# Group norm taken out of the chunk scan of a hybrid decoder layer, with paired first tiles at the projections' seams

## What is computed

```python
def ssd_mixer(xbc, dt_raw, z, h0, dt_bias, a_log, d_skip, g_norm, pad_front, chunk):
    ...
    y, h_last = ssd_scan(padt(xs), padt(dt), A, padt(Bm), padt(Cm), h0g, chunk)
    y = y[:, pad_front:pad_front + T] + d_skip...[:, :, None] * xs
    y = y.reshape(b, T, D_INNER) * jax.nn.silu(z.astype(f32))
    yg = y.reshape(b, T, SSD_GROUPS, D_INNER // SSD_GROUPS)
    yg = yg * lax.rsqrt(jnp.mean(yg * yg, axis=-1, keepdims=True) + EPS)
    y = yg.reshape(b, T, D_INNER) * g_norm.astype(f32)
    ...
mixed = jax.nn.sigmoid(ga) * (attn @ w_attn_out) + jax.nn.sigmoid(gs) * (ssd @ w_ssd_out)
x = x + mixed @ w_o
```

## Time and profile before

| what | value |
|---|---|
| median of 3 runs | 3813.21 us (3798.59 to 3815.85) |
| the profiled execution | 3804.04 us |
| its span from first to last instruction | 3802.2 us |
| PE busy | 3588.9 us (94%) |
| DVE, POOL, ACT busy | 2041.8, 1532.0, 811.5 us |
| mean granted TensorE clock | 0.951 of full speed |
| chain that ended last, by engine | PE 85%, DVE 6%, ACT 4%, issue 2%, DMA 1%, POOL 1% |

### The profile page before, as it was taken

One profiled execution on the slowest core, in us unless ns is written; L12 is line 12 of the kernel. 1 busy time (PEld: TensorE's weight loads), 2 busy tenths in 40 slices (PEclk: granted clock), 3 DMA queues, 4 the chain that ended last, 5 costly groups with the idle time before them and its releaser, 6 DMA issues.

```text
span 3802.2 us, 57123 instructions
## 1 busy us (share of the span) xinstructions
PE 3588.9 (94%) x22343; PEld 3397.6 (89%) x22343; DVE 2041.8 (54%) x3192; ACT 811.5 (21%) x1634; POOL 1532.0 (40%) x678
## 2 busy tenths in 40 slices
PE   7999999988999999996789989998999899999998
PEld 7999999988959999996789767668999799999998
DVE  5343333365759999876456534893165433433334
ACT  2000000022231111334565324662210200000000
POOL 2534435323313444442385004774433245344351
PEclk9999999999989999998799876999999999999999
DMA  2111111112202222222531215763242011111111
GB/s 86 56 39 44 55 33 54 45 45 62 59 28 84 89 95 80 98 89 62 69 112 51 66 42 132 190 163 117 96 143 71 23 50 55 39 44 55 33 55 56
DMA packets 399860, 272.33 MB, mean 72 GB/s; under 512 B 61850, under 2 KB 375538, under 8 KB 399736
## 3 DMA queue, kind: packets, MB, share of 16 engines
q1 hardware_dynamic: 379912, 225.76, 21.6%
q10 hardware_dynamic: 19824, 44.95, 3.1%
HBM read 211.05 MB, written 59.81 MB: 71 GB/s over the span
## 4 chain that ended last, share of the span: by engine, by line
PE 85%; DVE 6%; ACT 4%; issue 2%; DMA 1%; POOL 1%; SPq 1%; ACTq 0%; DVEq 0%; POOLq 0%
PE setA L349 10%; PE setA L350 10%; PE setA L351 10%; PE setB L349 9%; PE setB L350 9%; PE setB L351 9%; PE bankC L349 2%; PE bankC L351 2%; PE bankC L350 2%; PE bankD L351 2%; PE bankD L349 2%; PE bankD L350 2%; PE bankC L1417 2%; PE setA L1435 2%; PE setB L1435 2%
## 5 line engine op out<-in xcount | busy, mean ns | idle before, releaser
L341 POOL TENSOR_TENSOR whi<-wraw,ones 128x1024 fp32r<-128x1024 f32 x192 | 464.3, 2418 | 1688.2 <-PE setA L351 1078.3
L349 PE MATMUL setA<-hhi,whi 128*128 128x352 f32 (+1 forms) x2304 | 758.9, 329 | 43.2 <-issue 15.0
L350 PE MATMUL setA<-hlo,whi 128*128 128x352 f32 (+1 forms) x2304 | 751.2, 326 | 0.0
L351 PE MATMUL setA<-hhi,wlo 128*128 128x352 f32 (+1 forms) x2304 | 749.9, 325 | 0.0
L349 PE MATMUL setB<-hhi,whi 128*128 128x352 f32 (+1 forms) x2304 | 746.3, 324 | 0.0
L350 PE MATMUL setB<-hlo,whi 128*128 128x352 f32 (+1 forms) x2304 | 742.3, 322 | 0.0
L351 PE MATMUL setB<-hhi,wlo 128*128 128x352 f32 (+1 forms) x2304 | 741.1, 322 | 0.0
L349 PEld LDWEIGHTS setA<-hhi,whi 128*128 128x128 f32 x2304 | 441.1, 191 | 52.1 <-issue 25.8
L344 POOL TENSOR_TENSOR wlo<-wraw,whi 128x1024 fp32r<-128x1024 f32 x192 | 473.3, 2465 | 15.0
L350 PEld LDWEIGHTS setA<-hlo,whi 128*128 128x128 f32 x2304 | 441.0, 191 | 2.0
L351 PEld LDWEIGHTS setA<-hhi,wlo 128*128 128x128 f32 x2304 | 440.6, 191 | 0.0
(11 more groups left out here) (415 smaller groups left out, 5835.6 us busy)
## 6 DMA issues: line engine op xcount, KB each, us to landing
wraw<-in_w_in SPq DMA_DIRECT2D x64, 512.0 KB, 3.6
wraw<-in_w_ffn_gate SPq DMA_DIRECT2D x44, 512.0 KB, 3.7
wraw<-in_w_ffn_up SPq DMA_DIRECT2D x44, 512.0 KB, 3.7
wraw<-in_w_ffn_down SPq DMA_DIRECT2D x44, 512.0 KB, 3.5
abc<-acsD SPq DMA_DIRECT2D x8, 2048.0 KB, 9.8
xcD<-cv ACTq DMA_DIRECT2D x24, 520.0 KB, 2.7
xc<-xcD SPq DMA_DIRECT2D x8, 1536.0 KB, 14.4
zD<-spill ACTq DMA_DIRECT2D x16, 524.0 KB, 2.7
```

Of the source, the lines that this page charges most:

```text
L341: pool.tensor_tensor(dst_cols(slot, hi), dst_cols(slot), ones[:, :].unsqueeze(1).to_broadcast([P, KD, P]), ALU.mult).then_inc(w_hi, 1)
L349: pe.matmul(out, w1, r1, start=start, stop=False)
L350: pe.matmul(out, w1, r2, start=False, stop=False)
L351: return pe.matmul(out, w2, r1, start=False, stop=stop)
```

## The change

- `norm` leaves the scan. ACT copies the sums of squares of every chunk into rows `sums` (4 groups by 1048 tokens), and after the scan it takes two roots of 2 x 1048 elements a partition. DVE takes two reciprocals of the same size, each behind two of the state copies.
- y is written over z in `zc`; `y2` and `ss4` go. z has a semaphore of its own (`z_loaded`) that only the first `gate` of a chunk waits for. SP's `turn` loads `abc`, `xc` and `tc`, stores y unnormalised, waits until the store has landed, and then loads z.
- The 8 sample tokens aren't normalised on their own either: their root, reciprocal and product go, and their sums join `sums`.
- `dve_rows` multiplies `sraw` by gain and reciprocal in place (24 instructions for a half), ahead of the seam. The rounding at the seams is then one instruction a piece on ACT and one on DVE.
- The second `sraw` load is issued after the second SO weight load instead of the fourth.
- `gemm_pair` makes the first two tiles at all three seams, and waits for the second split only ahead of its second tile.
- Some semaphores of the sample part become the engine's common chain; ACT's loop over chunks is written out.

The diff, cut to what the text speaks of:

```diff
@@ -369,11 +369,13 @@
 
         def gemm_pair(pe, n, q, ready, between=None):
 
-            pe.wait_ge(w_split, n + 2)
+            pe.wait_ge(w_split, n + 1)
             for c, (o, w) in enumerate(CH):
                 if ready is not None:
                     pe.wait_ge(ready[0], ready[1] + c + 1)
                 for j in range(2):
+                    if j and c == 0:
+                        pe.wait_ge(w_split, n + 2)
                     if q:
                         pe.wait_ge(gemm_evac[j], 3 * (q - 1) + c + 1)
                     for k in range(KD):
...
@@ -1650,8 +1649,6 @@
             act.wait_ge(s_sc, 2 * NS + 2)
             act.activation(ps_[:, 0:PAST + 1], ss_[:, 0:PAST + 1], ACT.Exp, bias=smn[:, 0:1], scale=-1.0,
                            accum_out=smn[:, 1:2]).then_inc(s_relu, 1)
-            act.wait_ge(ys_ss, 2)
-            act.activation(rss[:, :, :], rss[:, :, :], ACT.Sqrt, bias=eps[:, 0:1], scale=1.0 / GW).then_inc(smp_act, 1)
...
-            v.wait_ge(smp_act, 2)
-            ch.run(v.reciprocal(rss[:, :, :], rss[:, :, :]))
-            v.tensor_tensor(ys[:, :, :].rearrange("p (g k) b -> p g k b", g=SG),
-                            ys[:, :, :].rearrange("p (g k) b -> p g k b", g=SG),
-                            rss[:, :, :].unsqueeze(2).to_broadcast([P, SG, GB, NS]), ALU.mult).then_inc(smp_norm, 1)
...
-        a = Region(AR, mboff - AR)
-        y2 = a.take("y2", [P, 2, NXB, P])
-        a = Region(mboff, AEND - mboff)
-        a.cur += DI * 4
-        zc = a.take("zc", [P, 2, NXB, P])
+        zc = at("zc", [P, 2, NXB, P], F32, mboff + DI * 4)
+        sums = at("sums", [P, SG, T], F32, mboff + DI * 4 + 2 * NXB * P * 4)
...
@@ -1885,46 +1874,53 @@
                 sp.dma_start(xc[slot][:, :, 0:w], xcD.rearrange("(b p) t -> p b t", p=P)[:, :, ts])\
                     .then_inc(chunk_loaded[slot], 16)
 
-            def load_rest(c, slot):
+            def load_tok(c, slot):
                 o, w = tok0(c)
-                ts = bass.ds(o, w)
-                sp.dma_start(tc[0:w, slot, :], tokD[ts, :]).then_inc(chunk_loaded[slot], 16)
-                sp.dma_start(zc[:, slot, :, 0:w], zD.rearrange("(b p) t -> p b t", p=P)[:, :, ts])\
-                    .then_inc(chunk_loaded[slot], 16)
-
-            def load(c, slot):
-                load_in(c, slot)
-                load_rest(c, slot)
-
-            def step(c, slot, used, nxt):
+                sp.dma_start(tc[0:w, slot, :], tokD[bass.ds(o, w), :]).then_inc(chunk_loaded[slot], 16)
+
+            def load_z(c, slot):
                 o, w = tok0(c)
-                sp.wait_ge(norm_ready, c * SG + SG)
-                sp.dma_start(sD.rearrange("(b p) t -> p b t", p=P)[:, :, bass.ds(o, w)], y2[:, slot, :, 0:w])\
+                sp.dma_start(zc[:, slot, :, 0:w], zD.rearrange("(b p) t -> p b t", p=P)[:, :, bass.ds(o, w)])\
+                    .then_inc(z_loaded[slot], 16)
+
+            def store_rows(c, slot):
+                o, w = tok0(c)
+                sp.dma_start(sD.rearrange("(b p) t -> p b t", p=P)[:, :, bass.ds(o, w)], zc[:, slot, :, 0:w])\
                     .then_inc(slot_out[slot], 16)
+
+            def turn(c, slot, used, nxt):
+
+                sp.wait_ge(y2_ready, c * SG + SG)
+                if nxt is not None:
+                    load_in(nxt, slot)
+                    load_tok(nxt, slot)
+                store_rows(c, slot)
+                if nxt is not None:
+                    sp.wait_ge(ysq_ready, c * SG + SG)
+                    sp.wait_ge(slot_out[slot], used * 16 + (SSD_OUT1 + 16))
+                    load_z(nxt, slot)
...
+            turn(0, 0, 0, 2)
             with sp.Fori(0, (NCH - 3) // 2) as i:
-                sp.wait_ge(y2_ready, i * 8 + 8)
-                load(i * 2 + 3, 1)
-                step(i * 2 + 1, 1, 0, None)
-                sp.wait_ge(y2_ready, i * 8 + 12)
-                load(i * 2 + 4, 0)
-                step(i * 2 + 2, 0, 0, None)
-            step(NCH - 2, 1, 0, None)
+                turn(i * 2 + 1, 1, i, i * 2 + 3)
+                turn(i * 2 + 2, 0, i + 1, i * 2 + 4)
+            turn(NCH - 2, 1, 0, None)
+            turn(NCH - 1, 0, 0, None)
             load_ao(sp, 2)
-            step(NCH - 1, 0, 0, None)
+        rs23 = at("rs23", [P, 2, T], F32, AR + 2 * XB)
...
             def ssq_copy(c, g, slot):
                 w = width(c)
                 wait_u(act, ssq_done, c, g, 0)
-                if g == 0 and not (isinstance(c, int) and c < 2):
-                    act.wait_ge(norm_ready, c * SG - SG)
-                act.activation(ss4[:, slot, g, 0:w], bankD[:, 0:w], ACT.Identity).then_inc(ssq_copied, 1)
-                if g == SG - 1:
-                    act.wait_ge(ssq_copied, c * 4 + 4)
-                    act.activation(ss4[:, slot, :, 0:w], ss4[:, slot, :, 0:w], ACT.Sqrt, bias=eps[:, 0:1],
-                                   scale=1.0 / GW).then_inc(root_done, 1)
+                o, _ = tok0(c)
+                act.activation(sums[:, g, o:o + w], bankD[:, 0:w], ACT.Identity).then_inc(ssq_copied, 1)
...
+            act.activation(sums[:, :, L:T], rss[:, :, :], ACT.Identity).then_inc(rss_in, 1)
             exps(0, 0, 0, 0)
-            over_chunks(act, step)
+            for c in range(NCH):
+                step(c, c % 2, c // 2, c + 1 if c < NCH - 1 else None)
             part_high(2, 4 * NCH)
             ssq_copy(NCH - 1, SG - 2, 0)
             square(NCH - 1, SG - 1, 0)
             ssq_copy(NCH - 1, SG - 1, 0)
+            act.wait_ge(ssq_copied, 4 * NCH)
+            act.wait_ge(rss_in, 1)
+            for h, dst in enumerate((sums[:, 0:2, :], rs23[:, :, :])):
+                act.activation(dst, sums[:, 2 * h:2 * h + 2, :], ACT.Sqrt, bias=eps[:, 0:1], scale=1.0 / GW)\
+                    .then_inc(root_done, 1)
...
-                if g == 0 and not (isinstance(c, int) and c < 2):
-                    v.wait_ge(slot_out[slot], used * 16 + SSD_OUT1)
+                if g == 0:
+                    v.wait_ge(z_loaded[slot], used * 16 + 16)
                 bs = slice(GB * g, GB * g + GB)
-                v.tensor_tensor(y2[:, slot, bs, 0:w], SETS[s][:, 0, :].rearrange("p (b t) -> p b t", t=P)[:, :, 0:w],
+                v.tensor_tensor(zc[:, slot, bs, 0:w], SETS[s][:, 0, :].rearrange("p (b t) -> p b t", t=P)[:, :, 0:w],
                                 zc[:, slot, bs, 0:w], ALU.mult).then_inc(y2_ready, 1)
 
...
-            def norm(c, slot):
-
-                w = width(c)
-                v.wait_ge(root_done, c + 1)
-                v.wait_ge(y2_ready, c * 4 + 4)
-                v.reciprocal(ss4[:, slot, :, 0:w], ss4[:, slot, :, 0:w]).then_inc(rstd_ready, 1)
-                v.wait_ge(rstd_ready, c + 1)
-                for g in range(SG):
-                    bs = slice(GB * g, GB * g + GB)
-                    v.tensor_tensor(y2[:, slot, bs, 0:w], y2[:, slot, bs, 0:w],
-                                    ss4[:, slot, g:g + 1, 0:w].to_broadcast([P, GB, w]), ALU.mult).then_inc(norm_ready, 1)
...
-                    if g == 2 and not (isinstance(c, int) and c == 0):
-                        norm(c - 1, 1 - slot)
...
-            norm(NCH - 1, 0)
-            for m in range(NXB // 4):
-                v.wait_ge(fin_done, m + 1)
-                v.tensor_copy(fin_st[:, m, :, :], CD[m % 2][:, :].rearrange("p (b n) -> p b n", n=P))\
-                    .then_inc(fin_evac, 1)
+            v.wait_ge(slot_out[1], Y_OUT0[1])
+            for h, t_ in enumerate((sums[:, 0:2, :], rs23[:, :, :])):
+                for m in (2 * h, 2 * h + 1):
+                    v.wait_ge(fin_done, m + 1)
+                    v.tensor_copy(fin_st[:, m, :, :], CD[m % 2][:, :].rearrange("p (b n) -> p b n", n=P))\
+                        .then_inc(fin_evac, 1)
+                v.wait_ge(root_done, h + 1)
+                v.reciprocal(t_, t_).then_inc(rstd_ready, 1)
...
             for m in range(KD):
                 load_tile(sp, TILE_SO + m, 0, m % 2, col_tile(so[0:D, :], m * P))
-                if m == 3:
+                if m == 1:
                     sp.wait_ge(part_ready, 6)
                     sp.dma_start(sraw[:, :, :], sD[D:2 * D, :].rearrange("(k p) t -> p k t", p=P)).then_inc(sraw_loaded, 16)
...
             for s in (1, 2, 3):
                 n, q = (TILE_AO + 8 * s, PART_ORD[s])
-                for m in range(2):
-                    gemm_tile(pe, n + m, q, m, ready=(part_ready, 3 * s) if m == 0 else None)
+                gemm_pair(pe, n, q, (part_ready, 3 * s))
                 with pe.Fori(0, 3 if s < 3 else 2) as i:
                     for j in range(2):
                         gemm_tile(pe, i * 2 + (n + 2 + j), i + (q + 1), j)
...
-        def act_high(act, s, c):
+        def act_high(act, s, src, c):
 
             o, w = CH[c]
-            act.wait_ge(mix_ready, 3 * (KD - 1) + c + 1)
+            if s < 3:
+                act.wait_ge(rows_ready, 3 * (s - 1) + c + 1)
+            else:
```

(40 more changed lines are left out.)

50 lines of the change are left out of this document (24 added, 26 removed).

## The result

The change takes **3775.5 us** (median of 4 runs, 3770.4 to 3781.8), the kernel before 3814.0 beside it: ratio 0.9909 (95% interval 0.9879 to 0.9938). In a later group of runs it took 3780.4 against 3803.1, ratio 0.9936 (0.9919 to 0.9954). It is faster by 0.6 to 0.9%. The profiled executions differ by less than the first medians (38.5 us): 3804.04 - 3776.31 = 27.7 us.

The account below looks back on a forecast made before the run. Scan bound by PE's work plus the wait for input. 27.9 + 1.0 + 1.5 + 7.0 - 8.6 + 4.6 + 5.6 = 39.0 us took the profiled 3804.0 to 3765.0, carried to the median as 3774; range 3755 to 3797.

Parts of the forecast that it names:

- The forecast case: Whole kernel: the terms come as summed, median 3774 us, own range 3762 to 3785; chance 55%.
- Scan, 27.9: Scan's 22 steps: `front` no longer waits for z, so PE keeps 6.57 us a step; 27.9 us gained.
- The 0.7 us kept for the boundaries: Scan: loss still allowed at the six chunk boundaries together, in case the input lands later; 0.7 us.
- The rival that DVE and POOL would hold PE at 7.0 us a step: Scan: without the norm's pause DVE and POOL slow PE, 9 us lost; chance 17% together with late input.
- z's room, 7 us: Scan: z, loaded behind the store, lands at 25.5 us of the turn, its first `gate` comes at 32.9.
- Start 1.0, last step 1.5, end 7.0: Scan: 1.0 us gained at ACT's first exponential, 1.5 from last-step table loads, 7.0 before and on the first projection tiles.
- Behind the scan, nothing: After the scan: wide reciprocals, state copies, `sraw` and row scaling cost nothing, with 20 us of cover.
- SSD seams, -4.3 each: Two SSD seams: B0 waits for the second split, third tile at E + 32.6; 4.3 us lost each, -8.6 together.
- The bound of -5.7: SSD seams: lower bound of the term, if `sraw`, queued ahead of the third tile's weights, comes late too.
- `w_o` seam, +4.6: `w_o` seam: pairing starts the third tile at 2910.8 instead of 2915.4; 4.6 us gained (2 to 5).
- Last pair of `w_o`, +5.6: Last `w_o` pair: A0 fills 3.84 of the 4.96 us split wait and the clock holds; 5.6 us gained.
- DVE and POOL excluding each other: SBUF rule: VectorE with both inputs in SBUF and GpSimd exclude each other for a whole instruction; spoke against the pairs.

Follow-up runs that it names:

- z_own: The kernel before, with z on its own semaphore that only a chunk's first `gate` waits for, norm kept in the scan: 3802.5 us against 3804.9, ratio 0.9989.
- no_norm: The kernel before without the reciprocals and products of the prompt's norm, ACT's roots and the wait for z kept: 3789.9 us against 3804.9, ratio 0.9964.
- front_z: The change, with a chunk's first `front` waiting for z again: 3851.6 us, ratio to the kernel before 1.0126.
- rows_late: The change, with DVE scaling the second half's rows only once the third tile's weights are split: 3767.6 us, ratio to the kernel before 0.9901.
- unpaired: The change with single tiles at the two SSD seams, the pair kept at the `w_o` seam: 3751.2 us, ratio to the kernel before 0.9855.
- pair_wait: The kernel before with only `gemm_pair` edited, waiting for the second split just ahead of the second tile: 3799.9 us against 3803.1, ratio 0.999.
- singles: The change with single tiles at all three seams and the second `sraw` load behind the fourth tile's weights: 3752.7 us, ratio to the kernel before 0.9868.
- split_first: The change with its pairs, but at the SSD seams DVE starts the second piece's `hlo` after the second split: 3760.4 us, ratio to the kernel before 0.9881.

## Why the prediction was right, and where it wasn't

The time (3774, measured 3775.5), the range and the direction were right. The forecast case, the one with 55%, is the one that came. That the time was met within 2 us is luck, though. The sum was too large: 39.0 us against the profiled execution, and the profile shows 27.7 (30.8 without the later input). The median before lay high in its first group (3814, later 3803 to 3805), and this covered the difference. Most of the excess lies at the seams: the SSD seams lost 7.6 us more than forecast, clock included, and the `w_o` seam gained 5.0 less. Point by point:

- **Scan, 27.9.** 28.7 in the same 22 steps. The 0.7 us kept for the boundaries wasn't lost. The number was right and half of its explanation wrong. "DVE can keep that pace" held only without the norm, and "the scan is bound by PE's work plus the wait for the input" was false: DVE with its norm needed 31.1 us a chunk; the 6.30 and 5.8 that I quoted already give 31.0. With the waits for ACT counted in every step it is 31.1. I counted the norm's removal as a thing that goes too, and gave it no price. `z_own` shows that the wait alone is worth nothing and `no_norm` that the norm alone is worth up to 2.8 us a chunk; together, with ACT's root gone too, they give 4.8. The rival that DVE and POOL would hold PE at 7.0 us a step didn't come, though POOL is at 30.15 of 31 us.
- **z's room, 7 us.** Shown: the first `gate` of a chunk doesn't wait, and z lands 7.3 us ahead of one. With the wait put back on `front`, a chunk takes 9.5 to 11.2 us more (`front_z`).
- **Start 1.0, last step 1.5, end 7.0.** 1.6 at the start. From the last `front` to the first AO tile 9.8, forecast as 1.5 + 8.2; on the AO tiles 0.3 lost, forecast 1.2.
- **The sixth step of the scan, not in the sum: 2.5.** See the last section. It depends on when the clock rises, which moved by more than this between two profiles of the change, so it is luck.
- **Behind the scan, nothing.** ACT's two roots took 2.05 and 2.03 us, and the whole of it cost PE nothing. Nor does the order of copies and reciprocals.
- **SSD seams, -4.3 each.** -4.5 at the second: B0 at E + 9.8, forecast E + 10.3, POOL's first part over at E + 4.7 as forecast. At the first seam -10.4, and 1.4 more for the clock behind the wait. The step that failed is "the third tile waits 1.3 us for its split, as behind the FFN's pair". It overlooked that `dve_rows` for the second half, 24 instructions of DVE, starts as soon as the second `sraw` has landed, right there. The bound of -5.7 had the right place and the wrong cause, and was passed: the weights behind `sraw` do come late (E + 23.8), but the pair's third tile frees its slot only at E + 27.6, so the scaling of the rows decided (`rows_late`). With single tiles the late weights decided (`unpaired`).
- **`w_o` seam, +4.6.** -0.4. The step that failed is "the preparation is unchanged". It was unchanged in code, and its phase was not: `hlo` came 0.02 us behind POOL instead of 1.6 ahead and took 5.3 us. With the other phase the seam gains 32.4 - 27.8 = 4.6 (`unpaired`). That this is the forecast to the tenth is luck too: with the code of before at this seam the third tile starts at E + 32.4 in the profile before and at E + 31.1 in those of `z_own` and `pair_wait`. The late phase came in all six profiles with pairs at the SSD seams and no fixed order, and in neither of the two of the change with single tiles there and no fixed order (`unpaired`, `singles`); what delays DVE's mixing there wasn't tried.
- **Last pair of `w_o`, +5.6.** 5.7, and 5.8 by itself in `pair_wait`.
- **DVE and POOL excluding each other** (the Trainium skill, SBUF — State Buffer, section "Who interferes with whom"). It spoke against the pairs, and the runs agree: the split's first half takes 2.41 us alone (`split_first`) against 4.38 beside an `hlo` (the change). The sum had used it where PE waits for a split, and neither for the scaling of the rows nor for the `hlo` that A0 waits for.

## What to carry to other kernels

An engine's busy time in a loop is not its need. Add up its own chain for one turn, waits for its partners included, and look at the distance between two starts of a thing that it does once a turn. Where this stays constant while another engine's wait for a load varies, suspect that the load is not the bound, and test it by removing that wait alone. Expect a second limit close behind the first: here each of the two removed alone gave 0 and 2.8 us a chunk, and the whole change 4.8.

Where two tiles share a right-hand side that is only just being made, ask which of two engines touches the memory first. Here pairing paid where the right-hand side came late in any case (`w_o`), and cost where a weight split would have been hidden behind the first tile (the SSD seams).
